# A two-layer hybrid model on one core: the first transposes quarter by quarter, and the short convolution's taps one place ahead of its tanh

## What is computed

```python
for l in range(DEPTH):                      # 2
    h = rms_norm(x, norm_w[l])
    p = h @ w_in[l]                         # 2048 x 6668
    qa, ka, va, za, ub, zb, qkv_c, b_c, a_c, zc = _split_cols(p)
    oa = sliding_window_sink_attention(...) * silu(za)      # mixer A
    ob = conformer_conv_module(ub, ...) * silu(zb)          # mixer B, 31 taps
    oc = gated_deltanet(qkv_c, b_c, a_c, ...)               # mixer C
    x = x + concatenate([oa, ob, norm(oc) * silu(zc)]) @ w_out[l]
```

## Time and profile before

| | us |
|---|---|
| median of 3 runs | 3556.43 |
| lowest, highest | 3553.24, 3559.59 |
| the profiled execution, its own time | 3560.55 |
| its span, first to last instruction | 3558.4 |
| TensorE busy in it (16098 matmuls) | 3429.6 |
| VectorE busy | 2288.7 |
| ScalarE busy | 1851.4 |
| GpSimd busy | 160.8 |

### The profile page before, as it was taken

One profiled execution on the slowest core, in us unless ns is written; L12 is line 12 of the kernel. 1 busy time (PEld: TensorE's weight loads), 2 busy tenths in 40 slices (PEclk: granted clock), 3 DMA queues, 4 the chain that ended last, 5 costly groups with the idle time before them and its releaser, 6 DMA issues.

```text
span 3558.4 us, 41522 instructions
## 1 busy us (share of the span) xinstructions
PE 3429.6 (96%) x16098; PEld 2771.7 (78%) x16098; DVE 2288.7 (64%) x3066; ACT 1851.4 (52%) x2528; POOL 160.8 (5%) x243
## 2 busy tenths in 40 slices
PE   7998999989999999999999999999999999999998
PEld 5777678767687877788888888877777888888886
DVE  4877565886666566566666666665665666666666
ACT  4564645555644365655454454543665555545544
POOL 3023000041000000000000000000000000000000
PEclk9999999999999999999999999999999999999999
DMA  6544355544355354456655655553544665565564
GB/s 195 159 127 126 107 165 169 159 122 124 107 179 163 106 156 133 150 182 188 190 187 184 191 185 185 190 161 102 158 137 154 194 190 186 180 196 183 184 195 154
DMA packets 399091, 578.50 MB, mean 163 GB/s; under 512 B 25473, under 2 KB 222585, under 8 KB 398256
## 3 DMA queue, kind: packets, MB, share of 16 engines
q1 hardware_dynamic: 392544, 557.93, 51.0%
q0 software_dynamic: 5904, 16.75, 1.6%
q10 hardware_dynamic: 448, 1.18, 0.1%
HBM read 570.78 MB, written 4.98 MB: 162 GB/s over the span
## 4 chain that ended last, share of the span: by engine, by line
PE 83%; DVE 9%; ACT 5%; issue 2%; DMA 1%; DVEq 0%; ACTq 0%; SPq 0%
PE PS L710 80%; PE PS L707 3%; DVE WL L1872 3%; ACT WH L1326 1%; DMA RAW<-in_w_in 1%; DVE AR L2012 1%; DVE ZA L2063 1%; DVE AR L2344 0%; ACT ZA L1396 0%; ACT AR L1680 0%; ACT L1596 0%; DMA X<-in_x 0%; ACT AR L1352 0%; DVE AR L2016 0%; DVE AR L2234 0%
## 5 line engine op out<-in xcount | busy, mean ns | idle before, releaser
L1872 DVE TENSOR_TENSOR WL<-RAW,WH 128x1024 fp32r<-128x1024 f32 x1056 | 1293.8, 1229 | 968.7 <-ACT WH L1326 965.7
L1326 ACT ACTIVATE WH<-RAW 128x1024 fp32r<-128x1024 f32 x1056 | 1105.9, 1056 | 1058.9 <-PE PS L710 675.2
L710 PE MATMUL PS<-WH,Ah 128*128 128x512 f32 x3520 | 1426.4, 405 | 35.9 <-DVE WL L1872 26.9
L710 PE MATMUL PS<-WL,Ah 128*128 128x512 f32 x3520 | 1382.2, 393 | 0.0
L710 PE MATMUL PS<-WH,Al 128*128 128x512 f32 x3520 | 1382.0, 393 | 0.0
L710 PEld LDWEIGHTS PS<-WH,Ah 128*128 128x128 f32 x3520 | 667.5, 190 | 207.4 <-issue 38.1
L710 PEld LDWEIGHTS PS<-WL,Ah 128*128 128x128 f32 x3520 | 666.8, 189 | 143.9
L710 PEld LDWEIGHTS PS<-WH,Al 128*128 128x128 f32 x3520 | 668.4, 190 | 136.6 <-issue 6.7
L710 PE MATMUL PS<-WH,Zh 128*128 128x512 f32 x704 | 278.6, 396 | 0.6
L710 PE MATMUL PS<-WL,Zh 128*128 128x512 f32 x704 | 274.5, 390 | 0.0
L710 PE MATMUL PS<-WH,Zl 128*128 128x512 f32 x704 | 274.3, 390 | 0.0
(11 more groups left out here) (320 smaller groups left out, 2148.6 us busy)
## 6 DMA issues: line engine op xcount, KB each, us to landing
RAW<-in_w_in SPq DMA_DIRECT2D x368, 512.0 KB, 3.7
RAW<-in_w_up SPq DMA_DIRECT2D x704, 256.0 KB, 3.1
RAW<-in_w_down SPq DMA_DIRECT2D x176, 512.0 KB, 4.0
RAW<-in_w_out SPq DMA_DIRECT2D x64, 512.0 KB, 3.7
RAW<-in_w_o SPq DMA_DIRECT2D x64, 512.0 KB, 3.7
RAW<-in_w_in SPq DMA_DIRECT2D x64, 256.0 KB, 3.0
AR<-in_c POOLq DMA_DIRECT2D x2, 1600.0 KB, 8.0
AR<-bias_scratch POOLq DMA_DIRECT2D x16, 192.0 KB, 4.0
```

The source lines that it names most:

```text
L710: return T.matmul(o, lhs, rhs, start=start, stop=stop, skip_group_check=True)
L1326: act(WH[:, j % NW, 0:n], raw_view(j), ACT.Copy).then_inc(*w_hi())
L1872: tt(WL[:, j % NW, 0:w], raw_view(j), WH[:, j % NW, 0:w].bitcast(F32), SUB).then_inc(*w_lo())
```

## The change

Three edits. **Round 0**: X comes in four column quarters (rows of 2 KB) with a semaphore each, and SyncE issues the first three weight tiles between them. The transposes, squares and gains of quarter c wait for 2c places more, so quarter 0 goes through alone and quarters 1 to 3 are worked two tiles apart between the first chunk's tiles; they use PSUM banks as the later rounds do. **Taps and tanh**: a `yield` between the taps and the tanh on ScalarE, between the taps and the product of silu on VectorE, and, for the qkv chunks, one before the flag on TensorE.

```diff
-        ident_in, x_in, prm0_in, prm_in = sem("ident_in"), sem("x_in"), sem("prm0_in"), sem("prm_in")
+        ident_in, prm0_in, prm_in = sem("ident_in"), sem("prm0_in"), sem("prm_in")
+        x_in = [sem(f"x{c}_in") for c in range(4)]
...
         def gt_index(r, c, q):
-            return 8 * r + (4 * q + c if r == 0 else 2 * c + q)
+            return 8 * r + 2 * c + q
...
                 if r == 0:
-                    T.wait_ge(x_in, 32)
+                    for _ in range(2 * c):
+                        yield
+                    T.wait_ge(x_in[c], 16)
                     if c == 0:
                         T.wait_ge(*u_dve.at("prm0"))
-                    turn_x(c, 0, 4 + c)
-                    yield
-                    T.wait_ge(*p_gt.at(gt_index(r, c, 0)))
-                    turn_x(c, 1, 4 + c)
-                    yield
                 else:
                     yield
                     T.wait_ge(*x_added.at(x_index[r] + c))
-                    if c > 1:
-                        T.wait_ge(*p_gt.at(gt_index(r, c - 2, 1)))
-                    for q in R2:
-                        turn_x(c, q, 4 + 2 * (c % 2) + q)
-                    yield
+                if c > 1:
+                    T.wait_ge(*p_gt.at(gt_index(r, c - 2, 1)))
+                for q in R2:
+                    turn_x(c, q, 4 + 2 * (c % 2) + q)
+                yield
...
                     yield from e.until("prm")
+                if n in conv4 + conv2:
+                    yield
                 e.flags.add(done)
...
             def prepare(r, c):
-                if 0 < r < 6:
-                    yield
                 if r == 0:
-                    A.wait_ge(x_in, 32)
-                else:
+                    for _ in range(2 * c + 1):
+                        yield
+                    A.wait_ge(x_in[c], 16)
+                elif r < 6:
+                    yield
+                if r > 0:
...
-                if r < 6:
+                if 0 < r < 6:
                     yield
...
                         act(Q[:, q0 + c, :], ptile(s, c), ACT.Copy, scale=P(("ccw", l), 54 + q0 + c)).then_inc(*e_act(f"{k}.k{c}"))
+                    yield
                     A.wait_ge(*e_dve.at(f"{k}.d3{w - 1}"))
                     act(TMF[:, 0:256 * w], flat(Q[:, q0:q0 + w, :]), ACT.Tanh).then_inc(*e_act(k + ".th"))
...
-                if r == 0:
-                    if c == 3:
-                        sum_squares(r)
-                    yield
-                    for q in R2:
-                        gain_x(r, c, q, 4 + c)
-                        yield
-                else:
-                    yield
-                    yield
-                    if c == 3:
-                        sum_squares(r)
-                    for q in R2:
-                        gain_x(r, c, q, 4 + 2 * (c % 2) + q)
-                    yield
+                for _ in range(2 * c + 1 if r == 0 else 2):
+                    yield
+                if c == 3 and r > 0:
+                    sum_squares(r)
+                for q in R2:
+                    gain_x(r, c, q, 4 + 2 * (c % 2) + q)
+                if c == 3 and r == 0:
+                    sum_squares(r)
+                yield
...
                             stt(Q[:, q0 + c, d:256], ptile(s, c)[:, 0:256 - d], P(("ccw", l), 18 * (3 - d) + q0 + c),
                                 Q[:, q0 + c, d:256], MUL, ADD).then_inc(*e_dve(f"{k}.d{d}{c}"))
+                    yield
                     q = flat(Q[:, q0:q0 + w, :])
...
         def sp_program():
-            for t in R2:
-                Y.dma_start(X[:, t, :], a["x"][0, 128 * t:128 * t + 128, :]).then_inc(x_in, 16)
+            def load_x(c):
+                o = slice(512 * c, 512 * c + 512)
+                Y.dma_start(X[:, :, o], a["x"][0, :, o].rearrange("(t p) n -> p t n", p=128)).then_inc(x_in[c], 16)
+
+            load_x(0)
             for j, (mat, segs, width, row, kp) in enumerate(plan):
+                if 1 <= j < 4:
+                    load_x(j)
```

More of the change, by code:

```diff
@@ L1340, in prepare @@
             def prepare(r, c):
-                if 0 < r < 6:
+                if r == 0:
+                    for _ in range(2 * c + 1):
+                        yield
+                    A.wait_ge(x_in[c], 16)
+                elif r < 6:
                     yield
-                if r == 0:
-                    A.wait_ge(x_in, 32)
-                else:
+                if r > 0:
                     A.wait_ge(*x_added.at(x_index[r] + c))
```

## The result

| | before | after |
|---|---|---|
| median | 3557.36 (4 runs) | 3533.65 (4 runs) |
| lowest, highest | 3553.24, 3559.59 | 3531.43, 3536.15 |
| profiled execution, its span | 3560.55, 3558.4 | 3536.15, 3534.0 |

The ratio is 0.9936 [0.9924, 0.9949]: 23.7 us faster, where 20.5 were forecast. The profiled executions lie 24.4 us apart.

A forecast was written before the change was run, and what follows sets the result against it. TensorE was taken as the bound, busy 3429.6 of 3558.4 us, leaving 128.8 without matmuls plus lowered-clock losses. Terms 9 + 6 + 5 + 2 - 1.5 = 20.5 us less gave 3536; range 3526 to 3549.

The forecast's parts named there:

- A: Rival at the start: clock stays at 1.2 GHz through the first chunk, four more slow tiles, 10 us; 3546, chance 0.15.
- B: Rival at the start: clock at 1.2 GHz also through the second chunk, 13 us slower; 3570, chance 0.03.
- tile 6: First chunk: needs WH 8, waits behind last squares and rstd; Al at 36.5 us where TensorE is free at 35.
- slow tile 0: First chunk: the first weight tile runs at half clock and takes 5.1 us.
- D: Rival, nothing gained: X's quarters land late and WL only trades places; within 7 us of today, 3553, chance 0.04.
- C: Rival: the place mixers C and A lose is paid back; A's low halves miss tile 3; 3546, chance 0.15.
- Start, 9 us: First chunk: quarter 0 goes through alone, so the chunk ends 9 us earlier than 52.8; own range 6 to 11.
- I take 5.5: Start: the gains' load lands at 5.5 us, between bounds of about 4.5 and 9.3.
- Taps at qkv0 and qkv1, 6 us: Qkv0 and qkv1: next WL comes 2.3 us earlier, removing 4.3 us of waits plus 1.7 of slow clock.
- Norms, 5 us: Qkv2: mixer C's norms begin one place later, one more tile done in their chain's shadow; 5 us for two layers.
- Query copy, 2 us: Qkv3: WH goes before the tanh, so the query copy comes earlier; 1 us a layer, bounds 0 and 4.
- End of the layer, -1.5 us: Mixer A ends one place later while o0 starts where it did; costs 0.75 us a layer, bounds 0 and 5.

The follow-up runs named there:

- e1: The changed kernel without its taps part (no yield between taps and tanh), so the start alone; 7.9 us faster than the kernel before.
- e3: The changed kernel with qkv2's taps and tanh back in one place and mixer C's later place removed; runs from 3535.3 to 3544.6 us, 10 slower by the medians.
- e10: The changed kernel with qkv2's taps and tanh in one place, but mixer C keeping its later place; 3541.0 us.
- e4: The changed kernel with SyncE issuing nothing behind X's first quarter until the gains' load has landed; first chunk ends at 49.0 us, whole time not given.
- e5: The changed kernel with round 0's rstd made behind quarter 3's Ah instead of ahead; ratio 0.9936 to the kernel before.
- e9: The changed kernel itself, run again beside later experiments; 3533.79 us, ratio 0.9931 to the kernel before, profiled execution 3529.14.
- e8: The changed kernel with taps and tanh of qkv3 alone joined in one place again; 3535.13 us.
- e11: The changed kernel with one more yield between qkv2 and mixer C on TensorE, ScalarE and VectorE; 3530.35 us.
- e6: The changed kernel with one more place between qkv3's taps and tanh, so the query copy stands ahead of the tanh; 3532.35 us.

## Why the prediction was right, and where it was not

**Right:** what bounds the kernel, the kind of the effects at the start, at the taps and at the query copy, and the time: 3533.65 for 3536. That the time fits so well has luck in it, since a start that was put too high stands against a stretch behind qkv2 that was put too low, and one kernel's profiled executions lie up to 7 us apart. The clock rivals A and B did not come about. A wanted four more slow tiles, 48 matmuls. By the distances of the matmuls the first chunk had twelve steps at half rate, and 5 to 18 in the other seven executions with that start, against eleven before. The slow tile 0 came as forecast (4.5 us for 5.1), and so did one short stretch after it. The Trainium skill's warning (TensorE: Matmul & The Clock Gate, "HAM oscillation — how this bites in real kernels"), by which matmuls in pieces with load waits between are throttled again at each piece, was borne out in part. In the changed kernel the piece behind a wait of 2.3 us at tile 6 began at a granted clock of 0.50, those behind 0.8 us and behind none did not. In the twelve executions that have the early start, each of the nine waits of 2.2 to 4.7 us at tiles 2 and 6 had such a stretch at its end (3.4 us, in e1 and e3 6.8), and those of up to 1.8 us had none. The second chunk was never slow through. D is out by the 23.7 us. Of C, the first half is seen in e10: without the split of qkv2 the place is paid back in front of the norms. In the changed kernel it is paid back in part only, and its second half, Al late at tile 3, did not come.

**Start, 9 us.** Measured 6.9 in the pair of profiles; 6.3 as a mean over the eight executions. Two steps were off. "I take 5.5" for the gains' load: it was 7.5, and TensorE's wait for it 7.6 to 8.5 us in every run of this start but e4. The prediction read the rule of the Trainium skill (DMA: Bandwidth & Descriptors, "Queues, rings and completion order") as giving 9. The row lies between the two, and e4 shows only that SyncE's other loads are what delays it. The rule does not give the 9 by force either: it counts descriptors in a packet, and a reader must add how long one is with shorter rows. Then tile 6: the Al came at 37.5, not 36.5, and TensorE waited 2.3 us, not 1.5. The rstd that the prediction blamed hid a load of weights that was nearly as late (e5).

**Taps at qkv0 and qkv1, 6 us.** Measured 7.1, in every run with the split to 0.1 us; no wait is left. The mechanism holds. The size rests on one trace of before: 4.3 us are waits, and the second layer's stretch at half rate went with the longest of them. e1, which has taps and tanh joined but neither this wait of 2.1 us nor the stretch, takes 76.9 us there, 4.4 more than with the split. So the split is worth 4 to 7 us here.

**Norms, 5 us.** The size holds: what e3 takes away is 5.3 us in the tiles (8.7 against e9) and 8 to 10 in the medians and ratios. The place where it shows and one step do not. "The chain neither shrinks nor starts later in absolute time (ScalarE was 5 us blocked before it)" is wrong: against the end of qkv2 it ends 1.9 us later (50.0 for 48.1), since the WH ahead of the second square is now the next tile's and waits 2.9 us for its weights. So tiles 41 to 63 gained nothing and the squares' waits stayed at 10.0, where they should have shrunk. What the later place gives comes up to 60 us further on, in the waits for WL (3.2 us less) and at the query copy, where VectorE's full stretch ends. I had costed the place by TensorE's tile and not by VectorE's list.

**Query copy, 2 us.** e8 says 0 to 3.6. The wait itself is 12.8 us in e3, which has qkv3's split without qkv2's, the "about 13" of the forecast; the 3.0 more of the changed kernel (9.8) come with qkv2's, which the sum had booked under the norms.

**End of the layer, -1.5 us.** Not seen: around the start of o0 (tiles 97 to 112 of both layers) TensorE stood idle 7.8 us before and 8.1 after. No wait for Al at o0 is listed in either; the four of the whole span (3.8 us in both) lie in the second block. The first such waits at o0 come in e11, a place further.

**The clock.** The sum held 1.7 us for it outside the start. Matmuls that took less long make up 6.4 us of the pair's 24.4: none in the start, 2.8 at qkv0 and qkv1, 3.6 from qkv2 to o3. The last no step had, and by e9, which is busy another 5.5 us less, they need not belong to the change.

The forecast's 20.5 was thus 2 too high at the start, 1 too low at the taps, and 4.8 too low behind qkv2 (5.5 for 10.3), 3.6 of these being shorter matmuls.

## What to carry to other kernels

Where an engine waits for another in the middle of its list, let one unit of its other work stand between producer and consumer: the split was worth 4 to 7 us at the two chunks where it only freed WH and WL. A step moved later in the order costs in front of the chain that it starts and pays behind it, on the engine that is full there; look at both ends, for they can cancel (e10). Look also at what comes to stand inside the chain: here it was one copy whose weights were not there yet. And before shortening the longest wait, look what is hidden behind it: a round trip through DRAM took the place of the query copy at once (e6), and a load of weights that of the rstd (e5).

## What the runs showed of the hardware

Some of VectorE's instructions take longer while GpSimd computes. The same WL in the changed kernel, before GpSimd's tensor operations begin at 239 us and in the midst of them:

```profile
235.75 1.23 DVE L1873 TENSOR_TENSOR WL<-RAW,WH 128x1024 fp32r<-128x1024 f32 x1 [0.19 <-ACT WH L1326]
...
258.37 1.60 DVE L1873 TENSOR_TENSOR WL<-RAW,WH 128x1024 fp32r<-128x1024 f32 x1
```

That is 30% more, in the 52 us a layer in which GpSimd computes, the 24 us among them in which VectorE hardly rests; a pair of L2059 goes from 0.85 to 1.66 us. The taps, which read one operand from PSUM, stay as they are (4.77 us at 120, and in the midst of it

```profile
268.67 4.75 DVE L2007 SCALAR_TENSOR_TENSOR AR<-PS,PRM,AR 128x255 f32<-128x255 f32 x12
```

). No run here takes GpSimd's work away, so the cause is not shown by an experiment. The Trainium skill (SBUF — State Buffer, "Who interferes with whom") says that a VectorE instruction with two SBUF inputs contends with a GpSimd instruction that reads SBUF, and that one with at most one SBUF input does not, outside VectorE's two-port modes. The trace agrees with this pattern: WL has two such inputs, the taps one beside their scalar.

And one kernel's executions differ by up to 6 us (3529.14 to 3535.57 in e9) with the same order. Two profiles of the changed kernel, 7.0 us apart, have nearly the same idle time (110.8 and 109.3 us). Where the clock is halved changes from one to the next: its records of 0.50 sum to 74.8 and 64.6 us.
